# Hybrid attention and expert backbone: attention steps of one unit or of two, and the order of the token tiles in the first layer

## What is computed

```
hl = modulate(rmsnorm(xl)); hc = modulate(rmsnorm(xc))
oa = window_attention_sink(...)         # A: 4 heads, window of 128 and context, a sink
ob = dense_attention(...)               # B: 4 heads of 96 columns
oc = diff_combine(dense_attention(...)) # C: 8 score sets of 32 columns, o1 - lambda * o2 per head
od = dense_attention(...)               # D: 4 heads of 64 columns
xl = xl + gt_a * (concat(oa, ob, oc, od) @ w_out)
xl = xl + gt_f * expert_choice_ffn(modulate(rmsnorm(xl)))
```

## Time and profile before

| what | value |
|---|---|
| median of 3 runs | 2156.08 us (2155.17 to 2156.92) |
| profiled execution, first to last instruction | 2157.7 us |
| attention of layer 0, first scores to the start of its last projection | 273.0 to 594.1 us |
| attention of layer 1, likewise | 1398.2 to 1629.9 us |
| PE busy over the span | 1970.7 us (91%) |
| DVE, ACT busy over the span | 676.9 us (31%), 529.7 us (25%) |

### The profile page before, as it was taken

One profiled execution on the slowest core, in us unless ns is written; L12 is line 12 of the kernel. 1 busy time (PEld: TensorE's weight loads), 2 busy tenths in 40 slices (PEclk: granted clock), 3 DMA queues, 4 the chain that ended last, 5 costly groups with the idle time before them and its releaser, 6 DMA issues. The chain is left out here.

```text
span 2157.7 us, 27259 instructions
## 1 busy us (share of the span) xinstructions
PE 1970.7 (91%) x10878; PEld 931.5 (43%) x10878; DVE 676.9 (31%) x1753; ACT 529.7 (25%) x1220; POOL 156.9 (7%) x155
## 2 busy tenths in 40 slices
PE   5999989999979999999999899889996898887875
PEld 2436465555633332323323556465554333333322
DVE  3322345666650100101001632366666011110203
ACT  3211154565531000100100321166553010000001
POOL 1100010000010010020100201100000000000000
PEclk8999979999989999999999999999998899999998
DMA  9742020000189999999999302110008899999995
GB/s 352 287 161 81 0 79 1 1 2 1 40 322 414 425 365 418 380 391 419 363 414 420 137 20 78 23 57 1 1 1 342 361 427 426 427 426 427 427 427 213
DMA packets 90935, 515.66 MB, mean 239 GB/s; under 512 B 10594, under 2 KB 15628, under 8 KB 36540
## 3 DMA queue, kind: packets, MB, share of 16 engines
q1 hardware_dynamic: 84496, 493.29, 56.4%
q0 software_dynamic: 4416, 15.21, 2.4%
q10 hardware_dynamic: 1900, 5.43, 0.6%
HBM read 498.69 MB, written 15.20 MB: 238 GB/s over the span
## 5 line engine op out<-in xcount | busy, mean ns | idle before, releaser
L712 PE MATMUL psS<-arena 128*64 128x512 f32 (+9 forms) x4552 | 1136.0, 556 | 70.8 <-DMA arena<-in_w_up 23.1
L712 PEld LDWEIGHTS psS<-arena 128*64 128x64 f32 (+4 forms) x4552 | 450.0, 158 | 666.2 <-issue 585.1
L715 PE MATMUL psT<-ident,arena 128*128 128x128 f32 (+1 forms) x1036 | 171.6, 289 | 47.3 <-DVE arena L2053 13.2
L1930 DVE TENSOR_REDUCE mx<-psS 128x1 f32<-128x768 f32 (+2 forms) x200 | 165.5, 827 | 152.1 <-PE psS L712 150.4
L1281 ACT ACTIVATE arena<-psT 128x768 f32<-128x768 f32 (+7 forms) x261 | 150.3, 577 | 244.0 <-PE psT L715 230.3
L1281 ACT ACTIVATE arena<-psS 128x128 f32<-128x128 f32 (+5 forms) x158 | 61.8, 421 | 572.1 <-PE psS L712 527.9
L2106 DVE TENSOR_TENSOR arena<-arena,psS 128x512 f32<-128x512 f32 x32 | 20.5, 684 | 549.6 <-PE psS L712 549.6
L715 PEld LDWEIGHTS psT<-ident,arena 128*128 128x128 f32 (+1 forms) x1036 | 119.5, 144 | 147.3 <-issue 107.9
L712 PE MATMUL psT<-arena 128*32 128x512 f32 x1536 | 174.5, 595 | 0.0
L1281 ACT ACTIVATE arena<-psS,nb 128x768 f32<-128x768 f32 (+2 forms) x200 | 158.1, 794 | 1.4
L712 PE MATMUL psM<-arena 128*128 128x512 f32 x288 | 140.1, 608 | 0.0
(11 more groups left out here) (223 smaller groups left out, 1285.5 us busy)
## 6 DMA issues: line engine op xcount, KB each, us to landing
arena<-in_w_gate SPq DMA_DIRECT2D x117, 1024.0 KB, 12.7
arena<-in_w_up SPq DMA_DIRECT2D x116, 1024.0 KB, 18.2
arena<-in_w_down SPq DMA_DIRECT2D x116, 1024.0 KB, 17.7
arena<-in_w_mod SPq DMA_DIRECT2D x48, 1024.0 KB, 7.4
arena<-in_w_in SPq DMA_DIRECT2D x6, 2048.0 KB, 7.8
arena<-in_w_out SPq DMA_DIRECT2D x8, 512.0 KB, 7.7
arena<-in_w_out SPq DMA_DIRECT2D x2, 2048.0 KB, 15.1
normed_rows<-arena ACTq DMA_DIRECT2D x8, 512.0 KB, 8.1
```

The source lines that it names most:

```text
L712: return nc.tensor.matmul(o, lhsT, rhs, start=start, stop=stop)
L715: return nc.tensor.transpose(o, in_, ident[0:n, 0:n])
L1930: link(V.reduce_max(mx[:, par:par + 1], view(S, 0, P, 0, (512, 2), (1, n)), axis=AX.XY))
```

## The change

**Steps of two.** The plan has one step for each pair of units: PE scores units 2p and 2p+1 of pair p, turns the two units of pair p-1 and multiplies pair p-2 by the values. The order in a step is: scores of 2p, scores of 2p+1, turning of the even unit of p-1, values of p-2, early filling work, turning of the odd unit of p-1, late filling work, turns. For C's pairs (4 and 5, `DIFFERENTIAL`), whose units fill both score buffers, the second unit's scores stand behind the early filling work. `O_COUNT`, `Q_AT`, `T_AT`, `GATE_AT` and `BIAS_AT` are given anew for the eight steps of a tile.

**ACT and DVE.** ACT follows in the order exponential of 2p, copy of the even unit, exponential of 2p+1, copy of the odd unit; in C's steps the copy of the even unit stands ahead of both exponentials of 2p, and those of 2p+1 stand last. DVE does the reciprocals or the mixing of the odd unit of pair p-1 after the *first* slot's maximum of the step, and in C's steps mixes unit 2p right after its two maxima.

**Order of tiles.** In layer 0 the tiles go 2, 0, 1, 3, 4, 5. Streams that the experts' results are added to keep their old order (`STREAMS`).

```
-LAG = 2
-T_AT = 2
-Q_AT = {4: "A", 5: "B0", 6: "B1", 12: "D", 14: "C1"}
-GATE_AT = ((7, 9, 11, 13), (9, 11))
-BIAS_AT = ((3, 5), (7,))
-O_COUNT = {3: 1, 4: 2, 5: 2, 6: 1, 7: 2, 8: 1, 9: 3, 10: 1, 11: 3}
+GROUPS = TURNS // 2
+DIFFERENTIAL = (4, 5)
+T_AT = 1
+Q_AT = {2: "A", 3: "B0", 4: "B1", 5: "D", 6: "C1"}
+EARLY_GATE, LATE_GATE = 0, 1
+GATE_AT = (((3, LATE_GATE), (4, EARLY_GATE), (4, LATE_GATE), (5, EARLY_GATE)), ((4, EARLY_GATE), (5, EARLY_GATE)))
+BIAS_AT = ((1, 2), (3,))
+O_COUNT = {2: (0, 2), 3: (0, 1), 4: (2, 3), 5: (2, 3), 6: (0, 1), 7: (0, 2)}
...
-        TILES = [list(range(TT)), list(range(TC, TT))]
+        TILES = [[TC, *range(TC), *range(TC + 1, TT)], list(range(TC, TT))]
+        STREAMS = [sorted(tiles) for tiles in TILES]
```

PE's list:

```
+                for n, step in enumerate(PLANS[l]):
+                    pair, apart = step.scored, differential(step.scored)
+                    if pair:
+                        scores(2 * pair)
+                    if pair is not None and not apart:
+                        scores(2 * pair + 1)
+                    if step.turned is not None:
+                        turned_probabilities(n, 2 * step.turned)
+                    if step.valued is not None:
+                        values(step.valued)
+                    gate_rows((n, EARLY_GATE))
+                    for x in step.early:
+                        output_piece(*x)
+                    if apart:
+                        scores(2 * pair + 1)
+                    if step.turned is not None:
+                        turned_probabilities(n, 2 * step.turned + 1)
+                    if n in BIAS_AT[l]:
+                        router_bias(BIAS_AT[l].index(n))
+                    gate_rows((n, LATE_GATE))
+                    for x in step.late:
+                        output_piece(*x)
+                    for x in step.turns:
+                        turn(*x, values=2 * step.turned + 1)
...
+                    if n in TAIL:
+                        if TAIL[n] == 0:
                             pe.wait_ge(z["S"], (l * TT + len(tiles)) * TURNS)
+                            pe.wait_ge(z["oe"], 2 * halves_through(l, n_tiles - 2, 1))
                             pe.sem_inc(z["open"], 1)
```

ACT's and DVE's:

```
+                    if pair is not None and not apart:
+                        exponentials(2 * pair)
+                    if step.turned is not None:
+                        probabilities_out(2 * step.turned)
+                    if pair is not None:
+                        exponentials(2 * pair + (not apart))
+                    gate_out((n, EARLY_GATE))
+                    if step.turned is not None:
+                        probabilities_out(2 * step.turned + 1)
+                    if apart:
+                        exponentials(2 * pair + 1)
...
+                    for s, slot in slots[:1]:
+                        maxima(s, slot)
+                    after_scores(step.turned)
+                    for s, slot in slots[1:]:
+                        maxima(s, slot)
+                    if apart:
+                        mixed(2 * pair)
+                        for slot in UNIT_SLOTS[(2 * pair + 1) % TURNS]:
+                            maxima(2 * pair + 1, slot)
```

More of the change, by code:

```diff
@@ L1 @@
+import dataclasses
 import math
@@ L224, in turns_through @@
 def turns_through(plan, turn):
-    order = [("Q", 0, name) for name in Q_FIRST] + [x for entry in plan for x in entry[3]]
+    order = [("Q", 0, name) for name in Q_FIRST] + [x for step in plan for x in step.turns]
     last = max(i for _, i, _ in order)
@@ L1034, in last_logits @@
                         last.then_inc(z["lp"], 1)
[L1036 to L1070, removed]
-                                for h in range(2):
-                                    r0 = i % 2 * SLOTS + LAST_SLOT[u] - 1 + h
-                                    last = mm(psO[64 * h:64 * h + 64, (2 + u % 4 // 2) * P:(3 + u % 4 // 2) * P],
-                                              view(rr, 0, P, r0, (0, 64)), ident[:, :])
-                            last.then_inc(z["O"], 2)
-                        elif u == 12:
-                            pe.wait_ge(z["Oc"], shared_groups(l, i, 2))
-                            for c in range(2):
-                                a = QN + tiles[i] * QNW + (4 + c) * P
-                                last = tr(psO[:, (2 + c) * P:(3 + c) * P], ar[:, a:a + P])
-                            last.then_inc(z["Cf"], 1)
-                    if s in BIAS_AT[l]:
-                        router_bias(BIAS_AT[l].index(s))
-                    if s in GATE_AT[l]:
-                        n = GATE_AT[l].index(s)
@@ new lines, in turned_probabilities @@
+                def turned_probabilities(step, v):
+                    i, u = divmod(v, TURNS)
+                    s0 = i * SLOTS + LAST_SLOT[u]
+                    if 8 <= u < 12:
+                        pe.wait_ge(z["mixed"], (l * TT + i) * 4 + u - 7)
+                        s0 -= 1
+                    else:
+                        pe.wait_ge(z["P"], s0 + 1)
+                    if v:
+                        pe.wait_ge(z["PTa"], l * TT * TURNS + v)
+                        jobs = [x for p in PLANS[l][:step] for x in p.turns]
+                        if jobs:
+                            pe.wait_ge(z["me"], turns_through(PLANS[l], jobs[-1]))
+                    for n, (_, at) in enumerate(places_of(tiles[i], LAST_SLOT[u])):
+                        a = PB + s0 % 4 * NTOK + at
+                        last = tr(psT[:, n * P:(n + 1) * P], ar[:, a:a + P])
+                    last.then_inc(z["T"], 1)
@@ new lines, in turned_back, with gate_rows @@
+                def turned_back(pair):
+                    i = pair // GROUPS
+                    pe.wait_ge(z["Oc"], shared_groups(l, i, 2))
+                    for c in range(2):
+                        a = QN + tiles[i] * QNW + (4 + c) * P
+                        last = tr(psO[:, (2 + c) * P:(3 + c) * P], ar[:, a:a + P])
+                    last.then_inc(z["Cf"], 1)
+                def gate_rows(at):
+                    if at in GATE_AT[l]:
+                        n = GATE_AT[l].index(at)
```

275 lines of the change are left out of this document (157 added, 118 removed).

## The result

The changed kernel takes 2179.95 us (median of 4 runs, 2178.69 to 2180.43) against 2156.50 (4 runs too) for the kernel before: the ratio is 1.0115, 95% interval 1.0102 to 1.0128. The forecast had the sign but less than half of the size: +10.0 us, where the medians differ by 23.5 and the two traces' spans by 20.2 (2157.7 to 2177.9). The result lies 1 us above the upper end of the stated range, 2179. The 3 us between 20.2 and 23.5 belong to the trace of before: the time of a run is 1.8 us more than the span of its trace (2179.74 and 2177.9), so the traced execution of before took some 2159.5, 3.0 over its median. The prediction read 1.6.

A forecast was written before the change was run, and what follows sets the result against it. PE was taken to bound attention, so only its waits could change. Full tiles +10.2, layer 1's first tile +3.8, layer 0's first three -2.8 and tails -1.2 gave +10.0 us, a median of 2166; range 2149 to 2179.

The forecast's parts named there:

- the falling clock: Rival: bubbles close together in full tiles halve PE's clock, 2 us more per fall, 2175 in all; chance 0.12.
- Full tiles: Attention's full latent tiles, both layers: each +1.7 us from new waits of PE, +10.2 for six.
- steps 0 and 1: Start of a full tile, A's units: waits of 2.2 us together against 1.5 before, taken as +0.8.
- the turn "T": Two-tile turn in step 1: PE waits 1.1 us for ACT's copy of the odd unit just turned.
- C's steps: C's units in a full tile: 0.5 wait at unit 11, 0.7 to 0.8 in all as before, +0.1 us.
- steps 6 and 7: D's first pair in step 6 costs +1.1 us; step 7 and B's steps give back 0.3.
- The last tile of a layer: Each layer's last attention tile: taken like other full tiles, +1.7 us, with the tail -0.6 a layer.
- Layer 0's first three tiles: Layer 0's start: one latent tile of 56.5 us, then two context tiles of 39.0 each; 134.5 against 137.3, -2.8.
- Layer 1's first tile: Latent tile with no pieces to cover its waits: +3.8 us on 51.00, from +1 to +6.
- faster rival: Rival: tiles without pieces gain by two units scored ahead; 2135, or 2148 with half of each; chance 0.14.
- C1: Two-tile turn in step 6 of a full tile: waits 0.8 us for ACT's odd copy; bracket of about 1 expected.
- The bracket before unit 11's scores: C's steps of a full tile: PE waits 0.5 us there, as DVE mixes unit 9 between unit 10's maxima.

The follow-up runs named there:

- e12: Changed kernel with one throwaway product in each of the three waits of steps 0 and 1, in three full tiles: 2175.82 us, 1.0094 of before.
- e1: Changed kernel with layer 0's tiles in their old order, both context tiles first: 2176.85 us, 1.0111 of the kernel before.
- e8: Changed kernel with throwaway products of 128 columns in the waits at the start of each layer's first tile: 2170.33 us, 1.0062 of before.
- e2: Kernel before, steps of one unit, with only layer 0's tiles in the new order, latent tile first: 2156.76 us, 1.0014 of before.

## Why the prediction was wrong in size

**The step that failed** is the price of the clock: the forecast took a full tile at 1.00 on the ground that full tiles stand single waits of 0.8 now, and gave the falling clock 0.12 at 2175. The changed tile has three waits, 1.20, 0.81 and 1.10 us, one soon after the other, and e12 shows that they are what brings it down. The rival was the truth, and its price was short as well, because it stood for the full tiles only: the first latent tile lost most.

**Full tiles.** Forecast +1.7, measured +3.4 to +3.5 for three of them and +2.4 for the one behind the context tiles. By PE's own starts steps 0 and 1 cost +1.0, of which 0.2 is the turn "T" at the lower clock (forecast +0.8), the scores behind it +1.5 (0), C's steps +0.15 (+0.1), steps 6 and 7 +0.9 (+1.1 and -0.3): at a clock of 1.00 the tile is 60.2 to 60.3 (e12, e1), forecast 60.1. For steps 0 and 1 that is luck in part, since two errors cancel. The waits are 1.20 and 0.81 for 0.65 and 0.45, with "T" at 1.10 as forecast, 3.1 in all for 2.2; and the scores of two units in a row take 1.28 us (1526.74 to 1528.02), where the sum has 0.85 twice. That VectorE's row there is nearly as long as ScalarE's was missed too, and would have warned that an early copy alone mends little. The last tile of a layer has no turns of the next: with its tail it cost +0.4 and +0.2 where +1.1 was forecast.

**Layer 0's first three tiles.** Forecast -2.8, measured +2.4. The context tiles are right to 0.4 in their sum. The latent tile is 5.6 over: 55.4 at full clock in e8, 62.1 in the trace.

**Layer 1's first tile.** Forecast +3.8, measured +5.7, of which 2.0 is clock (e8: 54.7).

**The sum.** The tiles whose clock fell, four full ones and two first, are over the forecast by 0.7 + 1.8 x 3 + 5.6 + 1.9 = 13.6; less 0.4 in the context tiles and 1.6 in the last tiles and tails. The rest, 1.5 more ahead of attention and 2.8 less behind it, is of one execution: the first scores of layer 0 come between 271.3 and 274.5 in the traces of the kernels without filler. 10.0 + 13.6 - 2.0 - 1.3 = 20.3, measured 20.2. (One sum of the prediction is off: half of each term of its faster rival gives 2145, not 2148.)

**What the prediction named as its test** decided it: brackets of 1.10 and 0.77 ahead of "T" and C1, ended by ACT; a tile of 61.9, not 60.1; and "a clock under 1.00 in full tiles". The bracket before unit 11's scores is 0.33, not 0.5.

The case for the rival had been there in the kernel before: the earlier trace rows show 0.74, 0.92 and 0.90 in the tiles that wait longest, and the earlier trace rows one such fall, behind a wait of 1.81. Nor did its full tiles stand single waits: the one of the earlier trace rows has 0.29, 0.78 and 0.40 there, 1.5 us in all, and holds 1.00; the change made that 3.1. The Trainium skill, page "TensorE: Matmul & The Clock Gate", section "A second HAM failure mode: psum-queue depth-cycling", says that small idle times between groups of products can throttle the engine again. The traces here agree: 4.25 us for scores that take 2.75, with no single wait over 1.20 us in the tile, in nine tiles of ten, and none of it once the waits are filled.

## What to carry to other kernels

Before a change that gathers PE's waits in one place, add up the waits that come to stand close together, and do not look at the longest alone, and look in the same trace at what the clock did behind the like. Where such waits can't be removed, throwaway products in them are cheap to try: in the kernel before they gave the only gain over it that was found here, and they have to stand in the wait, not behind it. Compare several traces before a clock fall is priced. And after one holder of a wait is moved, read who ends it next before moving another: gains measured one by one did not add up here.

## What had not been expected of the hardware

The clock falls with PE recorded busy for 57.0 of 61.9 us of a tile, behind waits of 1.20, 0.81 and 1.10 us, and behind the same waits it once held (e1, 60.28 us). And where it falls differs between executions of one program: 0.74 and 0.81 in the kernel before's first tile, 1.00 and 0.94 in e2's, with 2.7 and 3.3 us between them.
